# Mixture-of-experts gathers that leave out empty slots, and results of the first 16 experts added inside the second half of the expert loop

## What is computed

```python
g_sel = argmax(g_logits); e_in = e_logits[g_sel]            # 4 groups, then 8 experts of the group
top_v, top_i = lax.top_k(e_in, 2)
gates = softmax(top_v) * g_w
y[token] = sum over its two experts of gate * (silu(x @ w_gate[e]) * (x @ w_up[e])) @ w_down[e]
x = x + y
out = rms_norm_2(x, norm_final)
```

## Time and profile before

| | us |
|---|---|
| median of 3 runs | 2157.78 (2157.72 to 2159.1) |
| profiled execution, whole | 2160.14 |
| its span, first to last instruction | 2158.3 |
| PE busy in the span | 2060.6 (95%) |
| DVE, ACT, POOL busy | 861.9, 571.7, 283.5 |
| mean granted PE clock | 0.990 of full speed |

### The profile page before, as it was taken

How to read it: one execution, slowest core, us unless ns; L and a number is a source line. 1 busy time by engine, 2 the same in 40 slices (tenths; PEclk the granted TensorE clock), 3 DMA queues, 4 the chain that set the end, 5 groups by cost and what they waited for, 6 DMA issues and landing times.

```text
span 2158.3 us, 37599 instructions
## 1 busy us (share of the span) xinstructions
PE 2060.6 (95%) x15542; PEld 1145.6 (53%) x15542; DVE 861.9 (40%) x1463; ACT 571.7 (26%) x1044; POOL 283.5 (13%) x272
## 2 busy tenths in 40 slices
PE   6999999999999999999999999999799999999997
PEld 4445655655434445543456454565456666666553
DVE  2225530555556642885465541244511111111114
ACT  2123322333663210432134221143011111111113
POOL 0014400432330012014000000000100000000002
PEclk9999999999999999999999999999899999999999
DMA  8201221122205027100113002101699999999996
GB/s 315 91 16 43 103 79 39 64 88 86 56 1 155 30 89 167 53 1 0 46 72 115 32 1 78 42 30 41 254 390 404 409 411 412 411 415 411 413 407 250
DMA packets 108899, 351.84 MB, mean 163 GB/s; under 512 B 18904, under 2 KB 58224, under 8 KB 95888
## 3 DMA queue, kind: packets, MB, share of 16 engines
q1 hardware_dynamic: 64272, 274.98, 32.8%
q0 software_dynamic: 14464, 53.61, 7.3%
q10 hardware_dynamic: 30080, 22.13, 3.2%
HBM read 310.46 MB, written 40.24 MB: 162 GB/s over the span
## 4 chain that ended last, share of the span: by engine, by line
PE 71%; DMA 15%; DVE 7%; ACT 4%; issue 1%; ACTq 1%; POOL 1%; DVEq 0%; POOLq 0%; SPq 0%; PEldq 0%
PE bank L643 27%; DMA y_of_slot<-HT 11%; PE bank L797 9%; PE bank L1325 7%; PE bank L649 6%; PE bank L1341 3%; ACT work L1429 3%; PE bank L823 2%; DMA work<-in_w_e_up_dram 2%; PE bank L1137 2%; DVE work L1936 1%; PE bank L932 1%; PE bank L717 1%; PE bank L937 1%; DVE O L1936 1%
## 5 line engine op out<-in xcount | busy, mean ns | idle before, releaser
L643 PE MATMUL bank<-slots,HT 128*128 128x512 f32 (+2 forms) x960 | 350.7, 522 | 1.7 <-DVEq L142 1.1
L643 PEld LDWEIGHTS bank<-slots,HT 128*128 128x128 f32 x960 | 170.5, 190 | 164.9 <-issue 159.5
L1429 ACT ACTIVATE work<-bank 128x512 f32<-128x512 f32 (+6 forms) x223 | 116.7, 528 | 422.1 <-PE bank L643 193.8
L1429 ACT ACTIVATE HT<-bank 64x256 f32<-64x256 f32 (+2 forms) x215 | 91.8, 432 | 455.3 <-PE bank L1325 220.1
L1429 ACT ACTIVATE work<-work 128x1024 f32<-128x1024 f32 (+7 forms) x199 | 158.6, 808 | 170.5 <-DVEq L142 88.4
L1325 PE MATMUL bank<-slots,HT 128*32 128x256 f32 x3136 | 172.6, 379 | 3.3 <-DVE HT L2637 1.2
L1325 PE MATMUL bank<-work,HT 128*32 128x256 f32 x3072 | 169.1, 379 | 0.8 <-DMA work<-in_w_e_up_dram 0.7
L643 PE MATMUL bank<-HT,slots 128*128 128x512 f32 (+2 forms) x432 | 167.4, 546 | 2.3 <-DVEq L1949 1.4
L2711 POOL TENSOR_TENSOR work<-work 128x1024 f32<-128x1024 f32 (+4 forms) x80 | 120.3, 1503 | 354.9 <-DVEq L142 249.8
L2642 DVE TENSOR_TENSOR HT<-HT,bank 64x256 f32<-64x256 f32 x97 | 41.1, 423 | 263.2 <-ACT HT L1429 262.8
L1325 PEld LDWEIGHTS bank<-slots,HT 128*32 128x32 f32 x3136 | 103.1, 110 | 71.1 <-issue 7.7
(11 more groups left out here) (286 smaller groups left out, 2605.6 us busy)
## 6 DMA issues: line engine op xcount, KB each, us to landing
slots<-in_w_e_gate_dram SPq DMA_DIRECT2D x17, 2048.0 KB, 18.0
slots<-in_w_e_up_dram SPq DMA_DIRECT2D x17, 2048.0 KB, 22.7
slots<-in_w_e_down_dram SPq DMA_DIRECT2D x17, 2048.0 KB, 23.5
work<-in_w_e_gate_dram SPq DMA_DIRECT2D x16, 2048.0 KB, 18.1
work<-in_w_e_up_dram SPq DMA_DIRECT2D x16, 2048.0 KB, 22.7
work<-in_w_e_down_dram SPq DMA_DIRECT2D x16, 2048.0 KB, 23.5
slots<-in_w_in_dram SPq DMA_DIRECT2D x9, 2048.0 KB, 8.3
slots<-in_w_ada_dram SPq DMA_DIRECT2D x6, 2048.0 KB, 14.8
```

The costliest lines, as they stand in the source:

```text
L643: ins = pe.matmul(bank, lhsT, rhs, start=(n == 0), stop=(n == len(pairs) - 1))
L1429: return act.activation(o, i, f, bias=bias, scale=scale, **more)
```

## The change

- The token numbers carry + 1 into the one-hot product, so that an empty slot comes out as 0; DVE turns it back by - 1 and adds 2048 to the empty ones (`EMPTY`), so that their index lies beyond the table. The gathers of `xn` are issued with a bound (`bounds_check`), and a row beyond it is left out.
- `slot_id` of a choice in a block below 16 is pushed beyond `y_of_slot`; a second list, `early_id`, does the opposite and points only at blocks below 16. `early_gates` and `late_gates` split `gates2` in the same way.
- In iterations 8 to 15 (experts 16 to 31), now written out on DVE and POOL, POOL issues for each of the 8 token tiles two gathers by `early_id`, and DVE adds them, times their gates, to the residual `O`. The two buffers `EARLY_ROWS` are cleared once before the loop.
- The 16 gathers after the loop use the new `slot_id` and leave out the rows beyond the bound.

```diff
-    put("token", r + P * np.arange(NT)[None, :])
+    put("token", 1 + r + P * np.arange(NT)[None, :])
...
+        EARLY = EXPERTS // 2
+        EARLY_LOOPS = EXPERTS // 4
+        early_gates, late_gates = col(2 * NT), col(2 * NT)
+        early_id = ctx.enter_context(nc.sbuf_tensor("early_id", [P, 2 * NT], U32))
+        EARLY_ROWS = [work[:, TAIL + x * D:TAIL + (x + 1) * D] for x in range(2)]
+        Y_ROWS = EXPERTS * CAP + SPARE * TG
...
             idle_products(banks[0], 4)
+            pe.wait_ge(early_added, 2 * NT)
             for n in range(4):
                 residual(n)
...
             bank = ringV.take(dve)
+            line(dve.tensor_scalar(EMPTY[0:CAP, :], bank[0:CAP, 0:BLOCKS], 0.0, 2.0 * T, ALU.is_equal, ALU.mult))
             for x in range(2):
-                line(dve.tensor_copy(index[x][0:CAP, :], bank[0:CAP, x:x + 1]))
+                stt(index[x][0:CAP, :], bank[0:CAP, x:x + 1], -1.0, EMPTY[0:CAP, x:x + 1], ALU.add, ALU.add)
             tell("pool")
-            line(dve.tensor_copy(token_list[0:CAP, 0:BLOCKS], bank[0:CAP, 0:BLOCKS]), ringV.free)
+            line(dve.scalar_tensor_tensor(out=token_list[0:CAP, 0:BLOCKS], in0=bank[0:CAP, 0:BLOCKS], scalar=-1.0,
+                                          in1=EMPTY[0:CAP, :], op0=ALU.add, op1=ALU.add), ringV.free)
...
-            copy(slot_id[:, :], SLOT)
+            ts(EARLIER, BLOCK_OF, float(EARLY), None, ALU.is_lt)
+            stt(slot_id[:, :], EARLIER, 2.0 * Y_ROWS, SLOT, ALU.mult, ALU.add)
+            ts(BEYOND, EARLIER, -2.0 * Y_ROWS, 2.0 * Y_ROWS, ALU.mult, ALU.add)
+            tt(early_id[:, :], SLOT, BEYOND, ALU.add)
+            tt(early_gates, gates2, EARLIER, ALU.mult)
+            tt(late_gates, gates2, early_gates, ALU.subtract)
+            line(dve.memset(work[:, TAIL:TAIL + 2 * D], 0.0))
...
+            with dve.Fori(0, EXPERTS // 2 - EARLY_LOOPS) as it:
                 for x in range(2):
+                    expert(it, x)
+            for i in range(NT):
+                for x in range(2):
+                    expert(EXPERTS // 2 - EARLY_LOOPS + i, x)
+                for x in range(2):
+                    dve.wait_ge(early_in[x], 16 * (i + 1))
+                    line(dve.scalar_tensor_tensor(out=O[:, i, :], in0=EARLY_ROWS[x], scalar=early_gates[:, x * NT + i:x * NT + i + 1],
+                                                  in1=O[:, i, :], op0=ALU.mult, op1=ALU.add), early_added)
...
                 pool.indirect_dma_start(row[0:n, :], None, xn_dram,
-                                        bass.IndirectOffsetOnAxis(ap=index[place][0:n, :], axis=0))\
-                    .then_inc(sem, 16)
+                                        bass.IndirectOffsetOnAxis(ap=index[place][0:n, :], axis=0),
+                                        bounds_check=T - 1, oob_is_err=False).then_inc(sem, 16)
+
+            def gather_rows(rows, at, to, arrived, below=Y_ROWS):
+
+                pool.indirect_dma_start(to, None, y_dram[0:below], bass.IndirectOffsetOnAxis(ap=rows[:, at:at + 1], axis=0),
+                                        bounds_check=below - 1, oob_is_err=False).then_inc(arrived, 16)
...
+            for i in range(NT):
+                for x in range(2):
+                    e = EXPERTS - 2 * EARLY_LOOPS + 2 * i + x
+                    pool.wait_ge(tokens_turned, e + 1)
+                    pool.tensor_copy(index[x][:, :], token_list[:, e + 2:e + 3]).then_inc(index_ready, 1)
+                    pool.wait_ge(index_ready, e + 1)
+                    gather_block(x, XG[x], rows_gathered[x])
+                    if x == 0:
+                        for stored in y_stored:
+                            pool.wait_ge(stored, 64 * (EARLY // 2 + 1))
+                        pool.wait_ge(early_added, 2 * i)
+                        for half in range(2):
+                            gather_rows(early_id, half * NT + i, EARLY_ROWS[half], early_in[half], EARLY * CAP)
...
-                    pool.indirect_dma_start(YG[2 * i + x], None, y_dram,
-                                            bass.IndirectOffsetOnAxis(ap=slot_id[:, x * NT + i:x * NT + i + 1], axis=0))\
-                        .then_inc(combined[i], 16)
+                    gather_rows(slot_id, x * NT + i, YG[2 * i + x], combined[i])
```

More of the change, by code:

```diff
@@ L559, in program @@
         OH, PICKED = cut(temp(2 * NT * EXPERTS), 2 * NT), cut(temp(2 * NT * EXPERTS), 2 * NT)
+        EMPTY = temp(BLOCKS)
         SPN, INC, KE, BEHIND, CN = temp(EXPERTS), temp(EXPERTS), temp(EXPERTS), temp(EXPERTS), temp(SPARE + 1)
         R1, R2, R3, RG = temp(NT), temp(NT), temp(NT), temp(NT)
-        INDEX, RANK_OF, KE_OF, BLOCK_OF, ROW_OF, SLOT, BEYOND = (temp(2 * NT) for _ in range(7))
+        INDEX, RANK_OF, KE_OF, BLOCK_OF, ROW_OF, SLOT, BEYOND, EARLIER = (temp(2 * NT) for _ in range(8))
         assert at_tail[0] <= 15 * T - TAIL
@@ L591, in program @@
         eps_col, other_half = col(1), col(NT)
+        EARLY = EXPERTS // 2
[4 more added lines that the diff above has]
+        Y_ROWS = EXPERTS * CAP + SPARE * TG
+        early_in, early_added = [sem(f"early_rows_in{x}") for x in range(2)], sem("early_rows_added")
         GATE_DIAGS = cut(work[:, 16 * D:16 * D + 2 * NT * P], 2 * NT)
@@ L2647, in _, with expert @@
             block_ready(tokens_ready)
-            with dve.Fori(0, EXPERTS // 2) as it:
-                for x in range(2):
[L2650 to L2657, removed]
+            def expert(it, x):
+                for g in range(TGS):
+                    dve.wait_ge(silu_ready, it * 6 + 3 * x + g + 1)
+                    hidden_of(g, hidden_ready)
+                dve.wait_ge(tokens_turned, it * 2 + x + 2)
+                block_ready(tokens_ready)
+                dve.wait_ge(y_stored[x], it * 64 + 64)
+                dve.wait_ge(down_full, it * 4 + 2 * x + 2)
+                dve.tensor_copy(YO[x][:, HALF:HALF + QW], DOWN_BANKS[1][:, 0:QW]).then_inc(y1_out, 1)
+            with dve.Fori(0, EXPERTS // 2 - EARLY_LOOPS) as it:
+                for x in range(2):
+                    expert(it, x)
[6 more added lines that the diff above has]
+                                                  in1=O[:, i, :], op0=ALU.mult, op1=ALU.add), early_added)
             spare = spare_count(dve)
@@ L2665, in _ @@
             for at in range(2 * NT):
-                ts(GATE_DIAGS[:, at, :], const("ident"), gates2[:, at:at + 1], None, ALU.mult)
+                ts(GATE_DIAGS[:, at, :], const("ident"), late_gates[:, at:at + 1], None, ALU.mult)
             line(dve.memset(ss[:, 0:2 * NT], 0.0))
@@ L2691, in _ @@
                     for x in range(2):
-                        stt(O[:, i, :], YG[2 * i + x], gates2[:, x * NT + i:x * NT + i + 1], O[:, i, :], ALU.mult, ALU.add)
+                        stt(O[:, i, :], YG[2 * i + x], late_gates[:, x * NT + i:x * NT + i + 1], O[:, i, :], ALU.mult, ALU.add)
                     dve.sem_inc(tile_added, 1)
@@ L2865, in _ @@
             hear("dve")
-            with pool.Fori(0, EXPERTS // 2) as it:
+            with pool.Fori(0, EXPERTS // 2 - EARLY_LOOPS) as it:
                 for x in range(2):
```

## The result

The changed kernel takes 2178.82 us (median of 5 runs, 2171.72 to 2182.73), the kernel before 2159.1 in the same job (5 runs, 2157.72 to 2164.24): ratio 1.0073, 95% interval 1.0054 to 1.0091. It was forecast 0.30% faster. The profiled execution is the fastest of its runs, 2171.72, so its trace shows 11.6 of some 16 to 20 us.

A forecast was written before the change was run, and what follows sets the result against it. PE's own work and the weights' DMA were taken as near-equal limits, the stores as a third. 2160.14 + 2.7 - 3.2 + 0 - 6 = 2153.6 profiled, 2151.3 as median, 0.30% faster; range 2145 to 2161.

The forecast's parts named there:

- pricing of rows on the DMA engines: Gathers in the loop: 0.0108 us a row, so 0.29 us a step less in first half, 0.33 more in second.
- First half: Experts 0 to 15: fewer token rows leave PE's own time as the limit, 277.3 to 274.1 us, -3.2.
- Second half, the wait: Expert 18: early gathers wait for expert 15's stores, DVE's additions wait for them, PE stalls once for 4 us.
- Second half, stores: Experts 16 to 31: early rows delay stores, the 4 us stall lets them catch up; 1.4 us of stalls kept.
- The rival of the stores' pace: From expert 16 on stores set the pace: second half 289.1, whole 2165, slower; chance 0.08 fully in force.
- Ahead of the loop: DVE's longer preparation takes 3.15 us, 0.48 of it hidden; PE's first product comes 2.7 us later.
- Combination: After the loop: 944 of 2048 rows remain, gathers are bound by POOL's issues, PE's last products end earlier: -6 us.
- rows beyond the bound are moved: All gathers with a bound: left-out rows cost as much as others, whole 2182 us; chance 0.05.
- POOL's issue doubles: Combination: an issue with a bound takes 1.9 us instead of 0.95, whole 2165 us; chance 0.05.

The follow-up runs named there:

- tokens_only: Kernel before with only the token gathers leaving out empty slots, no early gathers, late gathers moving all rows: 2163.86 us, ratio 0.9998.
- tokens_spread: tokens_only with the token of rank r put in row 6 (r mod 16) + r / 16, spreading empty slots: 2153.31 us, ratio 0.9967.
- change_spread: Changed kernel with only the spread slots added (rank r to row 6 (r mod 16) + r / 16): 2163.83 us, ratio 1.0008.
- early_from_14: Changed kernel with only the blocks of experts 0 to 13 counted as early: 2177.35 us, ratio 1.0070.
- early_turns_only: early_from_14 with the spread slots of tokens_spread and every row of the early gathers pushed out of range: 2159.74 us, ratio 0.9983.

## Why the prediction was wrong

- **The step that failed** is the pricing of rows on the DMA engines, 1.04 us of all 16 for a gather of 96 rows or "0.0108 us a row", and what was built on it: 0.29 us a step less in the first half, 0.33 more in the second. A mean over 16 engines is the price only where rows are left out evenly. With stretches of six rows the first half lost no row at all on the six fullest engines; the second lost none on the three fullest (at most 11 of 96 on the six) and gained its early rows (by estimate 1104 / 16 = 69 an engine, 12 us at 0.17). That the placing of the same rows decides is shown by tokens_only against tokens_spread (279.0 forecast for the second half, 296.5 measured, 279.4 in change_spread); which engine serves which row is inferred.
- **First half**, -3.2 forecast, -1.8 in the profile by PE's steps, but +1.1 counted from the weights (and tokens_only 0.9998). With spread slots it is 273.7 against 277.3: the gain that I forecast exists on even engines.
- **Second half, the wait** at expert 18: place and chain right, 4 us forecast, 14.9 measured. All three times in it (stores, early gather, token gather) were longer than forecast, as I had taken them from engines that run evenly; with spread slots the stall is gone. And it was no cost of its own: two kernels without it were as slow.
- **Second half, stores**: I let them catch up; they were the third form of the same debt (early_from_14's stalls). The rival of the stores' pace, 2165 in my sum, named the place but not the cause. That change_spread's second half, 279.4, comes so near the forecast's 279.0 is luck: the forecast is made of a stall of 4 us and 1.4 of stores, the run has no such stall but 0.4 us in every second step and some waits at its end.
- **Ahead of the loop**, +2.7 forecast: from the issue of expert 0's weights to PE's first product 33.0 us before and 35.7 after. Right; the stage ahead was 1.9 us shorter in this execution, so the first product is at 1548.76.
- **Combination**, -6 forecast, -5.4 measured (42.4 to 37.1). Its queue row and the last products answer to the earlier trace rows:

```profile
q0 software_dynamic: 2304, 3.87, 36.6%
```

```profile
2149.42 3.70 PE L1414 MATMUL bank<-work 128*128 128x512 f32 x8 [1.59 <-DMA work<-y_of_slot,slot_id]
...
2156.48 7.13 PE L1414 MATMUL bank<-work 128*128 128x512 f32 x16 [1.65 <-DMA work<-y_of_slot,slot_id]
```

  3.87 MB as forecast (3.9), in the 2304 packets of before, and an issue at 1.00 instead of 0.95. Right in mechanism and nearly in size.
- The rivals that rows beyond the bound are moved, and that POOL's issue doubles, fell by these rows.

Left open is why PE's products take 0.45 us longer once behind each pair of early gathers, also when no bytes are moved. In early_turns_only the weight loads pause for 0.40 to 0.46 us each time, from 0.01 to 0.02 us after POOL's second issue ends; the additions ended 3.2 us before, so it is not they. In the changed kernel (PE's weight load, DVE's additions, POOL's second issue):

```profile
1907.22 6.81 PEld L1333 LDWEIGHTS bank<-slots,HT 128*32 128x32 f32 x126
1908.09 2.60 DVE L2684 SCALAR_TENSOR_TENSOR O<-work,small,O 128x1024 f32<-128x1024 f32 x2
1912.91 1.00 POOL L2889 DMA_INDIRECT work<-y_of_slot,early_id  x1 [0.30 <-issue]
1914.43 3.59 PEld L1333 LDWEIGHTS bank<-slots,HT 128*32 128x32 f32 x66 [0.39 <-issue]
```

Also open is why the runs of the changed kernel lie 11 us apart where those of before lie 7.

## What to carry to other kernels

A transfer has landed when the slowest DMA engine is done with its share, so leaving out rows gains only if it relieves the fullest engine: look at how far the 16 completions of one DMA lie apart, before and after, not at bytes. If filled rows come first, deal them out over the engines' stretches; here that turned 0 and +0.7% into -0.3% and 0. When a stall disappears and the time stays, the resource behind it is the bound, and the next place that waits for it will show the same sum.

## What the runs showed of the hardware

- A gathered row beyond the bound still costs a packet of 4 bytes: 1456 packets for 13 gathers with 5.11 MB and with 3.40 MB; the small packet took 0.010 us of its engine, one of 4096 bytes 0.183.
- With empty slots at the end of 96 rows the 16 completions of a 2 MB load (up weights), at most 1.9 us apart before, drifted to 10 and more; with the filled rows dealt out over six-row stretches, and no early gathers, they stayed within 4.
- A gather of 96 or 128 rows issued with a bound took POOL 0.98 to 1.02 us instead of 0.93 to 0.95, whatever it moved (a few took 1.4 to 2.5, with a bound or without).
- After a wait of 9.8 us PE resumed at a granted clock of 0.50, the lower of its two levels: the products at 1879.24 to 1884.4 of the changed kernel.
